# Keeping the low parts of the weights in memory for the second token group

## The reference

```python
for l in range(DEPTH):                       # DEPTH = 2
    h = rmsnorm(x, gl[0])
    # layer 0: gated DeltaNet heads and spatial gating; layer 1: mLSTM heads
    mix = mixer(h @ w_in[l]) @ w_out[l]      # w_in 1024 x 3080, w_out 1024 x 1024
    x = x + rmsnorm(mix, gl[1])
    h = rmsnorm(x, gl[2])
    x = x + rmsnorm(square(relu(h @ w_ff1[l])) @ w_ff2[l], gl[3])   # 1024 x 4096, 4096 x 1024
```

## Time and profile before

| | |
|---|---|
| median of 3 runs | 2603.74 us (2602.95 to 2604.94) |
| the profiled execution | 2604.6 us, of which the span is 2602.9 us |
| TensorE busy | 2536.0 us (97%) |
| VectorE busy | 1381.0 us (53%) |
| ScalarE busy | 1114.2 us (43%) |
| GpSimd busy | 274.0 us (11%) |
| DMA moved | 321.45 MB, mean 123 GB/s |
| granted TensorE clock, mean | 0.992 of full speed |

### The profile page before, as it was taken

How to read it: one execution, slowest core, us unless ns; L and a number is a source line. 1 busy time by engine, 2 the same in 40 slices (tenths; PEclk the granted TensorE clock), 3 DMA queues, 4 the chain that set the end, 5 groups by cost and what they waited for, 6 DMA issues and landing times.

```text
span 2602.9 us, 39034 instructions
## 1 busy us (share of the span) xinstructions
PE 2536.0 (97%) x16187; PEld 2274.9 (87%) x16187; DVE 1381.0 (53%) x2205; ACT 1114.2 (43%) x1869; POOL 274.0 (11%) x438
## 2 busy tenths in 40 slices
PE   8998989999999999999999999999999999999999
PEld 7778888787878798899999999998887888999998
DVE  4756774755655575534444465535654466444344
ACT  6554446554454344433333345433333345323324
POOL 5121112100101011110000001111111000000000
PEclk9999999999999999999999999999999999999999
DMA  7554435533324265543433335554445443333232
GB/s 205 159 149 114 114 90 142 154 98 102 112 78 122 79 186 160 177 130 98 114 97 99 98 109 174 162 148 130 119 133 153 123 127 112 96 104 111 88 90 84
DMA packets 369393, 321.45 MB, mean 123 GB/s; under 512 B 12602, under 2 KB 340340, under 8 KB 369217
## 3 DMA queue, kind: packets, MB, share of 16 engines
q1 hardware_dynamic: 336224, 207.91, 27.8%
q0 software_dynamic: 32992, 111.06, 14.5%
HBM read 261.33 MB, written 57.58 MB: 123 GB/s over the span
## 4 chain that ended last, share of the span: by engine, by line
PE 82%; DVE 7%; ACT 5%; DMA 3%; issue 2%; POOL 0%; POOLq 0%; ACTq 0%; DVEq 0%
PE dense L624 74%; PE mixer L624 6%; DVE wlo L1766 2%; ACT arena L1245 1%; ACT whi L1245 1%; DVE ffh L1805 1%; DVE arena L1996 1%; DVE hf L1907 1%; ACT relu L1245 0%; DVE arena L1998 0%; ACT ffh L1245 0%; DVE hlo L1903 0%; PE mixer L690 0%; ACT L1245 0%; DMA arena<-xrow 0%
## 5 line engine op out<-in xcount | busy, mean ns | idle before, releaser
L624 PE MATMUL dense<-hhi,whi 128*128 128x272 f32 (+1 forms) x3072 | 846.7, 330 | 21.8 <-DVE wlo L1766 16.1
L624 PE MATMUL dense<-hhi,wlo 128*128 128x272 f32 (+1 forms) x3072 | 827.1, 324 | 0.0
L624 PE MATMUL dense<-hlo,whi 128*128 128x272 f32 (+1 forms) x3072 | 825.3, 323 | 0.0
L1766 DVE TENSOR_TENSOR wlo<-wst,whi 128x1024 fp32r<-128x1024 f32 x384 | 472.0, 1229 | 232.9 <-ACT whi L1245 232.0
L1245 ACT ACTIVATE whi<-wst 128x1024 fp32r<-128x1024 f32 x384 | 403.8, 1052 | 426.8 <-PE dense L624 414.3
L624 PEld LDWEIGHTS dense<-hhi,whi 128*128 128x128 f32 x3072 | 517.3, 189 | 77.4 <-DVE wlo L1766 22.5
L624 PEld LDWEIGHTS dense<-hhi,wlo 128*128 128x128 f32 x3072 | 515.0, 190 | 41.9
L624 PEld LDWEIGHTS dense<-hlo,whi 128*128 128x128 f32 x3072 | 517.2, 189 | 38.3 <-issue 0.7
L624 PE MATMUL dense<-h1hi,whi 128*128 128x272 f32 (+1 forms) x1536 | 423.5, 330 | 11.7 <-DVE wlo L1766 5.7
L624 PE MATMUL dense<-h1hi,wlo 128*128 128x272 f32 (+1 forms) x1536 | 413.9, 324 | 0.0
L624 PE MATMUL dense<-h1lo,whi 128*128 128x272 f32 (+1 forms) x1536 | 413.3, 323 | 0.0
(11 more groups left out here) (391 smaller groups left out, 1823.2 us busy)
## 6 DMA issues: line engine op xcount, KB each, us to landing
wst<-in_w_ff_dram SPq DMA_DIRECT2D x256, 512.0 KB, 4.0
wst<-in_w_in_even_dram SPq DMA_DIRECT2D x48, 512.0 KB, 4.1
wst<-in_w_in_odd_dram SPq DMA_DIRECT2D x48, 512.0 KB, 4.0
proj<-ffh POOLq DMA_DIRECT2D x48, 272.0 KB, 2.6
proj<-ffh POOLq DMA_DIRECT2D x48, 256.0 KB, 2.5
arena<-proj POOLq DMA_DIRECT2D x24, 512.0 KB, 4.9
out_dram<-arena POOLq DMA_DIRECT2D x17, 512.0 KB, 4.7
wst<-in_w_out_even_dram SPq DMA_DIRECT2D x16, 512.0 KB, 3.9
```

The costliest lines, as they stand in the source:

```text
L624: return pe.matmul(out, lhsT, rhs, start=start, stop=stop)
L1766: TT(wlo[:, u % 2, :], wst[:, u % 2, :], whi[:, u % 2, :].bitcast(F32), ALU.subtract)\
```

## The change

Units of group 0 (`stored`) work as before, and each low part made for them is also stored to a new tensor `wlow` in memory (192 blocks of 512 KB, written as 128 rows of 4 KB). Units of group 1 (`fetched`) fetch the block back into `wlo`; VectorE does nothing for them, and their loads and their first matmuls wait for `whi` alone instead of `w_split`. Both transfers are issued by SP, on the queue of the weight loads. A fetch for unit u waits until unit u - 1 has run its first matmul, and until every store issued so far has landed. In group 0 a `lo` waits for the landing of the store that last read its half of `wlo`.

```diff
+        self.stored, self.fetched = {}, {}
+        for u, (kind, l, g, a, k) in enumerate(self.units):
+            kept = self.fetched if g else self.stored
+            kept[u] = len(kept)
+        self.stored_at = {(kind, l, a, k): self.stored[u] for u, (kind, l, g, a, k) in enumerate(self.units) if not g}
...
+        wlow = nc.dram_tensor("wlow", (len(PLAN.stored), P, 1024), F32)
...
+        def split_wait(eng, u):
+
+            if u in PLAN.stored:
+                eng.wait_ge(S("w_split"), PLAN.stored[u] + 1)
+            else:
+                eng.wait_ge(S("w_hi"), u + 1)
...
+            sent = [0, 0]
+
+            def low_store(u):
+                sp.dma_start(wlow[PLAN.stored[u]], wlo[:, u % 2, :].bitcast(F32)).then_inc(S(f"w_kept{u % 2}"), 16)
+                sent[u % 2] += 1
+
+            def low_fetch(u):
+                kind, l, g, a, k = PLAN.units[u]
+                sp.wait_ge(S("w_used"), u)
+                for b in range(2):
+                    sp.wait_ge(S(f"w_kept{b}"), 16 * sent[b])
+                sp.dma_start(wlo[:, u % 2, :].bitcast(F32), wlow[PLAN.stored_at[kind, l, a, k]]).then_inc(S(f"w_low{u % 2}"), 16)
...
                 if u >= 2:
-                    sp.wait_ge(S("w_split"), u - 1)
+                    split_wait(sp, u - 2)
                 sp.dma_start(dst.rearrange("p (a b) -> p a b", a=src.shape[1]), src)\
                     .then_inc(S(f"w_loaded{u % 2}"), 16)
+                if u - 2 in PLAN.stored:
+                    low_store(u - 2)
+                if u - 1 in PLAN.fetched:
+                    low_fetch(u - 1)
...
+            low_fetch(len(PLAN.units) - 1)
...
                 if p == 0:
-                    pe.wait_ge(S("w_split"), u + 1)
+                    split_wait(pe, u)
+                    if u in PLAN.fetched:
+                        pe.wait_ge(S(f"w_low{u % 2}"), 16 * sum(v % 2 == u % 2 for v in PLAN.fetched if v <= u))
...
             def lo(u):
-                if u >= len(PLAN.units):
+                if u not in PLAN.stored:
                     return
                 dve.wait_ge(S("w_hi"), u + 1)
+                if u - 2 in PLAN.stored:
+                    dve.wait_ge(S(f"w_kept{u % 2}"), 16 * sum(v % 2 == u % 2 for v in PLAN.stored if v < u))
```

More of the change, by code:

```diff
@@ L810, in every_row @@
             def every_row(v, a):
-                pe.wait_ge(S("gs_rows"), 1)
+                pe.wait_ge(S("gs_spread"), 1)
                 return mm(v, spread4[:, :], a.rearrange("p a h -> p (a h)"))
@@ L838, in gdn_rows @@
                 elif step == "kT":
-                    pe.wait_ge(S("gs_rows"), 2)
+                    pe.wait_ge(S("gs_spread"), 2)
                     s(pe.transpose(bank(2), keys, ident[:, :]), "kT")
@@ L980, in gdn_sample @@
                 if step == "vo":
-                    pe.wait_ge(S("gs_spread"), 1)
+                    pe.wait_ge(S("gs_spread"), 4)
                     for k in range(2):
@@ L989, in gdn_sample @@
                     last.then_inc(S("g_vnew"), 1)
-                    pe.wait_ge(S("gs_qdm"), 1)
+                    pe.wait_ge(S("gs_spread"), 3)
                     for b in range(NB):
@@ L998, in gdn_sample @@
                 elif step == "u":
-                    pe.wait_ge(S("gs_spread"), 2)
+                    pe.wait_ge(S("gs_spread"), 5)
                     pe.wait_ge(S("g_ofa"), TILES + 1)
@@ L1119, in ml_sample @@
                         mm(MB[:, 0, 0:DV + 1], rows_of(m["ST"]), V1[:, 0, :], start=True, stop=False)
-                        pe.wait_ge(S("gs_qdm"), 2)
+                        pe.wait_ge(S("gs_spread"), 6)
                     else:
@@ L1127, in ml_sample @@
                                       start=r == 1 and b == 4, stop=b % 4 == 3)
-                    last.then_inc(S("ms_num"), 1)
+                    last.then_inc(S("ms_n"), 1)
                 elif step == "dc":
-                    pe.wait_ge(S("gs_spread"), 3)
+                    pe.wait_ge(S("gs_spread"), 7)
                     if r == 0:
@@ L1140, in ml_sample @@
                                       V1[rows_at(h), 0, 0:DV])
-                    last.then_inc(S("ms_dc"), 1)
+                    last.then_inc(S("gs_ds"), 1)
                 elif step == "end":
@@ L1657, in ml_sample @@
                 if step == "num" and r == 0:
-                    act.wait_ge(S("ms_num"), 1)
+                    act.wait_ge(S("ms_n"), 2)
                     A_(m["HN"][:, 0:DV + 1], MB[:, 0, 0:DV + 1], ACT.Copy).then_inc(S("ms_kept"), 1)
@@ L1662, in ml_sample @@
                     act.wait_ge(S("ms_nset"), 2)
-                    act.wait_ge(S("ms_dc"), 4)
-                    act.wait_ge(S("ms_n"), 2)
+                    act.wait_ge(S("gs_ds"), 6)
+                    act.wait_ge(S("ms_n"), 4)
                     A_(m["NROW"][0:NB * H], MB[0:NB * H, 2, 0:P], ACT.Copy)
@@ L1965, in gdn_prep @@
                                           mybir.AxisListType.X, ALU.add)
-                        dve.tensor_copy(heads_of(spread4[:, :]), bcm(ident[0:NS, 0:NS], [NS, H, NS]))                            .then_inc(S("gs_rows"), 1)
+                        dve.tensor_copy(heads_of(spread4[:, :]), bcm(ident[0:NS, 0:NS], [NS, H, NS]))                            .then_inc(S("gs_spread"), 1)
                         link(dve.tensor_reduce(rowmask[:, :], own[:, :, :], mybir.AxisListType.X, ALU.add))
@@ L2027, in gdn_rows @@
                     link(own_head(gcol[:, :], MB[:, 2, 0:6 * H].rearrange("p (a h) -> p a h", h=H), 6))
-                    dve.sem_inc(S("gs_rows"), 1)
+                    dve.sem_inc(S("gs_spread"), 1)
                     w("bc", 16 * (t + 1))
@@ L2059, in gdn_rows @@
                        colmask[:, :, :].unsqueeze(1).broadcast_to([P, H, NB, NS]), ALU.mult)\
-                        .then_inc(S("gs_qdm"), 1)
+                        .then_inc(S("gs_spread"), 1)
                     w("nw", 1)
@@ L2374, in ml_sample @@
                 elif step == "num" and r:
-                    dve.wait_ge(S("ms_num"), 2)
+                    dve.wait_ge(S("ms_n"), 3)
                     TT(m["HN"][:, 0:DV], m["HN"][:, 0:DV], MB[:, 0, 0:DV], ALU.add).then_inc(S("ms_kept"), 1)
                 elif step == "dc":
-                    dve.wait_ge(S("ms_dc"), r + 1)
+                    dve.wait_ge(S("gs_ds"), r + 3)
                     for b in (2 * r, 2 * r + 1):
```

## The result

The changed kernel takes 2653.78 us in the median (2648.91 to 2661.69, 4 runs) against 2604.31 us of the kernel before in the same comparison (2602.95 to 2604.94, 4 runs). The ratio is 1.0194 with a 95% interval of 1.0166 to 1.0221: slower by 49.5 us. That lies 16 us above the top of the predicted range. The direction was right and the size was not.

A forecast was written before the change was run, and what follows sets the result against it. TensorE was taken to bound the kernel, busy 2536.0 of 2602.9 us. Terms -5.2 + 12.5 + 4 + 1.5 = +12.8 us on the profiled 2604.6 gave 2617.4, hence a predicted 2616.5 us; range 2598 to 2638.

The forecast's parts named there:

- the relief: Group 1, VectorE freed of 192 low parts (236 us): TensorE's stalls shrink by 5.2 us, from about 2 to 12.
- The stall at 241 us: First section of group 1: TensorE's wait at line 2142 stays, 8.7 us instead of 7.2, gain 0.
- The stall at 351 us: First section of group 1: the 4.71 us `wlo` wait mostly returns at line 2142, about 4 us; gain 1.1.
- small waits: Section at 192 us: TensorE's 3.0 us of small waits for VectorE's mixer steps shrink by a third, gain 1.0.
- The fetch in steady state: Units of group 1: a fetch lands in 3.4 to 4.0 us, hidden by TensorE's own 6 us.
- late in general: Rival: throughout group 1 fetches take 6.0 us to land, costing 74 us, 2678 us in all; chance 0.14.
- The changes of groups: First fetch of group 1 behind load and store: late by 7.7, 3.6, 0.9 and 0.3 us; 12.5 together, 6 to 18.
- Bursts within group 1: Fetches behind slow weight loads in SP's queue: four late places, 6.9 us, taken as 4, from 0 to 15.
- The stores in group 0: Group 0: 101 MB of stores beside loads with time to spare slow GpSimd's mixer fetches; 1.5 us, between 0 and 6.
- The fetches: Group 1: hidden in most units, late only where groups change (12.5 us) and in bursts (4 us).

The follow-up runs named there:

- relief alone: Changed kernel with nothing stored, and group 1 neither making nor fetching low parts but multiplying with what lies in the buffer: 2598.52 us, 0.9986 of the kernel before.
- stores alone: Changed kernel, but group 1 makes its low parts on VectorE and fetches nothing: 2619.70 us without one outlying execution, ratio 1.0067, +16.5 us against the kernel before.
- kernel with fetches and 24 stores: Changed kernel storing only the first section's 24 blocks; all 192 fetches take one of them, mostly wrong blocks: 2628.74 us, 1.0101 of the kernel before.
- own-store kernel: Changed kernel, but a fetch waits for the landing of its own block's store, not all stores so far: 2646.44 us, 1.0166 of the kernel before.

## Why the prediction was wrong, step by step

**What bounds the kernel, and the relief: right in size.** TensorE, with a ceiling of 26 us in group 1, and 5.2 us to be gained. The relief alone measured 4.7, with an interval from 1 to 6. That the two numbers lie so close is partly luck: the one trace has the gain mostly in busy time, not in the stalls of the sum.

**The stall at 241 us: right in place.** It stands at 8.2 us where I said 8.7. With the relief alone it is 6.5, so without the fetches the chain did move up, by some 2 us, which the sum had at 0.

**The stall at 351 us: half right.** The wait did come back at line 2142, with 6.7 us where I said about 4, and a further 3.9 us appeared there at 306 us, which the sum did not have. I took the chain's trips through memory as "not moved" and forgot that the fetches share the DMA engines with them. The first section of group 1 had 2.1 us of gains in the sum (1.1, and 1.0 of small waits) and came out 5.3 us longer.

**The fetch in steady state: right.** I said 3.4 to 4.0 us; it is 3.7, and in the last section of 64 units, with little other traffic, all land in 3.3 to 4.8. That section is 406.4 us long against 406.1. The rival "late in general" did not happen: only 11 of TensorE's waits in dense work are of this kind.

**The changes of groups: right in mechanism, undersized.** Third: 10.3 for 7.7, because the load took 10.5 us instead of 8.5 and the fetch 4.2 instead of 3.4. Fifth: 3.6 for 3.6. The two small ones, 0.9 and 0.3, came to 1.5 and 1.1. Together 16.4 for 12.5.

**Bursts within group 1: undersized.** Taken at 4. The six waits for fetches away from the changes add up to 6.2 us, and the unit after the longest of them, at 1154.5 us, takes 1.5 us longer than before. The burst paragraph says 15 for the upper end, and the range has 12; with 15 it would end at 2641, still short of the result.

**The stores in group 0: this step failed.** "No row shows such a mixture; the price is between 0 and 6, and I take 1.5." The stores alone cost 16.5 us, nearly three times the upper end. With that in the place of 1.5 the sum is 28 us, and the time 2631.5, within the range. I had checked a store against the low part that must wait for it at the median pace of a quiet section, not in the first section, where loads of x, spills and projections run together. And I had no term for what stores do to GpSimd's transfers on which the mixers of group 0 wait, but the 2.8 us of state loads, which became 7.3.

**The fetches: the second step that failed.** "The fetch is hidden, by TensorE's own 6 us." In 181 of 192 units it is, and yet it costs, by what it does to the others. The sum had 12.5 + 4 = 16.5 us for fetches; with relief (-4.7) and stores (+16.5) measured, 49.5 + 4.7 - 16.5 = 38 us are left for them, in part together with the stores. This takes the time out of the range. What makes it up can be read from the profiled executions of the relief alone and of the kernel with fetches and 24 stores, 32.7 us apart: 12.2 us are waits for fetches, 9.0 us are added at line 2142 (24.1 against 15.1), and 11.7 us are busy time.

**The lower clock: a term put at nothing.** The sum has no price for what TensorE's clock does. In the profiled executions the changed kernel's TensorE is busy 12.1 us more for the same 16187 matmuls, at a mean granted clock of 0.984 against 0.992. The clock's record in the traces has TensorE busy at its lower level of 1.2 GHz for 60.9 us, against 35.8 us before. At half the speed the 25.1 us more cost 12.5 us, an estimate that accounts for the whole 12.1. So of the span's 44.3 us more, 32.2 are idle time and about 12 are clock. Only 4.3 of these were seen above, at the two long stalls. The timed executions agree: all four of the changed kernel have 0.984, and those of the kernel before in the experiments' comparisons 0.990 to 0.996.

**What stays open.** Relief -4.7, stores +16.5 and fetches with 24 stores +30.2 make 42 of 49.5 us. The 24 stores are in both of the last two, some 5 us by the first section's length (178.9 against 173.3 us with the relief alone). So about 12 us come only with stores and fetches together; the intervals of the four comparisons leave an error of some 10 us on that. The traces give it a place: with all stores the waits at the changes of groups are 16.4 us, with 24 stores 4.5. The own-store kernel takes 6 us back. How much of the fetches' cost away from the changes is their bytes, and how much their own lateness, isn't split.

The two failures with the traffic have one root, as I read it: I priced each transfer by the room for itself, and took the average DMA share as slack. Halving the bytes, with the number of transfers the same, took back 35% of the stores' 16.5 us and 47% of the 30.2 of the fetches and their 24 stores. More than half of either cost was left.

## What to carry to other kernels

Where the matrix engine is 97% busy, another engine's saving is worth at most the waits that name it, stall by stall: 236 us of VectorE were 4.7 us here. New traffic is paid by every transfer that something waits for, most of all in the stretches that are dense already: two sections hold 17 us of what the stores cost. Price it there, with the slow landings of the trace, and not by the mean share. Stalls that are added can also lower the granted clock behind them, which cost about 12 us here and wants a term of its own. A wait for all stores, ahead of the first fetch that reads any of them, puts two landings in series in front of the critical engine; letting each fetch wait for its own store alone took 8 us off TensorE's waits at the changes of groups, and 6 of the 49.5 us off the loss, while the bytes stayed the same.

## What the runs showed of the hardware

- A further 512 KB in rows of 4 KB behind a load and a store on one queue lands 1.3 us after the store (own-store kernel: 943.1, 944.4, 945.7), in a burst too. Issued by ScalarE on its own queue a fetch took 7.6 us in the burst at the same place.
- An SP store of 128 rows of 4 KB took 5.6 us to land in the median, the fetch of the same bytes 3.7.
- The transfers of `arow` and the stores of the projections, all on GpSimd's queue, went from 2.9 to 4.3 us and from 2.5 to 4.3 us to landing in the median, while SP's queue went from 27.8% to 50.1% of the engines' time.
- After stalls of 10.3 and 3.6 us the granted clock of the next unit was 0.73 and 0.68, and the units took 2.3 and 2.0 us longer than before. Over the whole span TensorE was busy at the lower level for 60.9 us instead of 35.8.
